# A two-block model layer: eight of twelve w_mod column blocks pre-summed on GpSimd, then summed over rows by TensorE

## The reference, cut to what matters

```
mod_x = jnp.split((jax.nn.silu(c) @ w_mod + b_mod)[:, None, :], 6, axis=-1)
mod_c = jnp.split((jax.nn.silu(c_ctx) @ w_mod + b_mod)[None, None, :], 6, axis=-1)
hc = modulate(rmsnorm(ctx, norm1_g), mod_c[0], mod_c[1])
hx = modulate(rmsnorm(x, norm1_g), mod_x[0], mod_x[1])
```

## Time and profile before

| | |
|---|---|
| median of 3 runs | 1835.47 us (1831.92 to 1836.16) |
| span of the profiled execution | 1824.3 us; no time of its own is recorded beside it |
| TensorE matmul / VectorE / ScalarE / GpSimd busy | 93% / 35% / 24% / 9% |
| mean granted TensorE clock | 0.969 |
| w_mod stage (first w_mod product to start of attention) | 105.75 to 202.04 us |

### The profile page before, as it was taken

One profiled execution on the slowest core, in us unless ns is written; L12 is line 12 of the kernel. 1 busy time (PEld: TensorE's weight loads), 2 busy tenths in 40 slices (PEclk: granted clock), 3 DMA queues, 4 the chain that ended last, 5 costly groups with the idle time before them and its releaser, 6 DMA issues.

```text
span 1824.3 us, 21872 instructions
## 1 busy us (share of the span) xinstructions
PE 1705.0 (93%) x8774; PEld 885.3 (49%) x8774; DVE 647.0 (35%) x1210; ACT 443.7 (24%) x775; POOL 170.2 (9%) x172
## 2 busy tenths in 40 slices
PE   7999999889999999999699998999799999999983
PEld 3455564545445555455355548975433333333331
DVE  3379111242223122221269947542522221222213
ACT  2233552214312122111258512331100000000001
POOL 0000000011111111110000023100111111111110
PEclk9999999989999999999899999999799999999997
DMA  9274611389999999999480091044799999999994
GB/s 367 93 257 160 213 70 47 133 321 407 392 401 411 407 400 406 407 411 413 174 322 1 5 143 47 1 162 194 277 392 403 406 409 407 406 421 408 417 414 175
DMA packets 94220, 515.26 MB, mean 282 GB/s; under 512 B 22429, under 2 KB 28157, under 8 KB 69544
## 3 DMA queue, kind: packets, MB, share of 16 engines
q1 hardware_dynamic: 82920, 496.46, 70.0%
q0 software_dynamic: 11200, 17.39, 2.9%
HBM read 506.09 MB, written 27.05 MB: 292 GB/s over the span
## 4 chain that ended last, share of the span: by engine, by line
PE 70%; DMA 15%; issue 7%; DVE 5%; SPq 2%; ACT 1%; DVEq 0%; POOLq 0%
PE bank L852 22%; PE bank L868 10%; PE bank L454 8%; PE bank L462 8%; DMA ring<-in_w_up 7%; DMA ring<-in_w_down 4%; PE bank L809 3%; PE bank L839 3%; PE bank L730 2%; PE bank L879 2%; PE bank L520 2%; PE bank L685 2%; PE bank L447 1%; DVE arena L2549 1%; DMA ring<-diag 1%
## 5 line engine op out<-in xcount | busy, mean ns | idle before, releaser
L854 PE MATMUL bank<-ring,arena 128*64 128x512 f32 x928 | 418.7, 605 | 0.0
L852 PE MATMUL bank<-ring,arena 128*64 128x512 f32 x752 | 339.1, 604 | 9.4 <-DMA ring<-in_w_up 6.8
L868 PE MATMUL bank<-ring,arena 128*64 128x512 f32 x544 | 247.9, 598 | 2.6 <-DMA ring<-in_w_down 2.6
L870 PE MATMUL bank<-ring,arena 128*64 128x512 f32 x544 | 247.9, 598 | 0.0
L2448 DVE TENSOR_TENSOR arena<-arena,bank 64x512 f32<-64x512 f32 x70 | 48.3, 690 | 560.5 <-ACT arena L1763 560.5
L454 PE MATMUL bank<-arena,ring 128*128 128x512 f32 x560 | 244.6, 593 | 0.0
L852 PEld LDWEIGHTS bank<-ring,arena 128*64 128x64 f32 x752 | 100.7, 139 | 208.5 <-issue 202.4
L852 PE MATMUL bank<-arena 128*64 128x512 f32 x368 | 166.1, 605 | 9.3 <-DMA ring<-in_w_up 5.0
L1429 POOL DMA_INDIRECT arena<-xnd,smalli x70 | 67.6, 966 | 1074.4 <-PE bank L839 536.0
L454 PEld LDWEIGHTS bank<-arena,ring 128*128 128x128 f32 x560 | 105.2, 190 | 127.2 <-issue 127.2
L1763 ACT ACTIVATE arena<-bank 64x512 f32<-64x512 f32 x70 | 41.2, 588 | 512.1 <-PE bank L854 512.1
(11 more groups left out here) (439 smaller groups left out, 1999.2 us busy)
## 6 DMA issues: line engine op xcount, KB each, us to landing
ring<-in_w_down SPq DMA_DIRECT2D x62, 2048.0 KB, 33.2
ring<-in_w_up SPq DMA_DIRECT2D x54, 2048.0 KB, 16.9
ring<-in_w_gate SPq DMA_DIRECT2D x45, 2048.0 KB, 17.4
arena<-in_w_gate SPq DMA_DIRECT2D x19, 2048.0 KB, 25.2
ring<-in_w_mod SPq DMA_DIRECT2D x12, 2048.0 KB, 8.0
ring<-in_w_in SPq DMA_DIRECT2D x10, 2048.0 KB, 15.7
arena<-in_w_up SPq DMA_DIRECT2D x10, 2048.0 KB, 29.8
ring<-in_w_out SPq DMA_DIRECT2D x4, 2048.0 KB
```

Source lines behind the costliest of these rows:

```text
L852: pe.matmul(GU[0:CAP, :], x, wg_[:, c, :], start=(c == 0), stop=(c == KD - 1), skip_group_check=True)
L854: mm = pe.matmul(GU[CAP:2 * CAP, :], x, wu_[:, c, :], start=(c == 0), stop=(c == KD - 1), skip_group_check=True)
L868: pe.matmul(Y[0:CAP, :], x, wd_[:, c, 0:512], start=(c == 0), stop=(c == 3), skip_group_check=True)
L870: mm = pe.matmul(Y[CAP:2 * CAP, :], x, wd_[:, c, 512:1024], start=(c == 0), stop=(c == 3), skip_group_check=True)
```

## The change

Of the twelve w_mod blocks, the eight whose columns only mod_x needs (2048 to 6143) are now taken first, and the four that both vectors need come last (`MOD`). For the first eight (`SUMMED`), GpSimd multiplies each of the 8 chunks of a landed block by that chunk's column of silu(c), in place, then adds chunks 4 to 7 onto 0 to 3, 2 to 3 onto 0 to 1, and 1 onto 0. TensorE then needs 4 products for the block instead of 32: the 128 partitions of chunk 0 against a stationary pair of columns, ones and zeros. It waits for GpSimd's sum first. The other four blocks go as before. The places move: blocks 6 and 7 (counted from 1) stand after the last q/k feature, blocks 8 to 10 behind the first value tile; 11 and 12 stay.

```diff
+        only_first = small(2)
-        for n, u in enumerate(U_MOD):
-            plain[u] = cols(a["w_mod"], n)
+        MOD = [4, 5, 6, 7, 8, 9, 10, 11, 0, 1, 2, 3]
+        SUMMED = 8
+        for i, u in enumerate(U_MOD):
+            plain[u] = cols(a["w_mod"], MOD[i])
...
-            def modulation(n0, n1):
+            def modulation(i0, i1):
-                for n in range(n0, n1):
-                    w = use(U_MOD[n])
+                for i in range(i0, i1):
+                    n = MOD[i]
+                    w = use(U_MOD[i])
                     b = V.deal(pe, f"mod{n}")
-                    for k in range(KD):
+                    if i < SUMMED:
+                        pe.wait_ge(S("mod_summed"), i + 1)
                         for g in range(4):
-                            mm = pe.matmul(b[32 * g:32 * g + 2, 0:P], chunks(cs, 2)[:, k, :], w[:, k, P * g:P * g + P],
-                                           start=(k == 0), stop=(k == KD - 1), skip_group_check=True)
+                            mm = pe.matmul(b[32 * g:32 * g + 2, 0:P], only_first, w[:, 0, P * g:P * g + P],
+                                           start=True, stop=True, skip_group_check=True)
+                    else:
+                        ...
-            pe.wait_ge(S("consts"), 3)
+            pe.wait_ge(S("consts"), 4)
...
-            modulation(5, 9)
+            modulation(5, 7)
...
-                    modulation(9, 10)
+                    modulation(7, 10)
...
-            sp.wait_ge(V.free, V.at("mod11"))
+            sp.wait_ge(V.free, V.at(f"mod{MOD[-1]}"))
...
+            pool.wait_ge(S("silu_c"), 1)
+            for i in range(SUMMED):
+                pool.wait_ge(*landed(U_MOD[i]))
+                w = unit(U_MOD[i])
+                for k in range(KD):
+                    pool.tensor_scalar(w[:, k, :], w[:, k, :], cs[:, 2 * k:2 * k + 1], None, ALU.mult)\
+                        .then_inc(S("mod_scaled"), 1)
+                pool.wait_ge(S("mod_scaled"), KD * (i + 1))
+                pool.tensor_tensor(w[:, 0:4, :], w[:, 0:4, :], w[:, 4:8, :], ALU.add).then_inc(S("mod_added"), 1)
+                pool.wait_ge(S("mod_added"), 2 * i + 1)
+                pool.tensor_tensor(w[:, 0:2, :], w[:, 0:2, :], w[:, 2:4, :], ALU.add).then_inc(S("mod_added"), 1)
+                pool.wait_ge(S("mod_added"), 2 * i + 2)
+                pool.tensor_tensor(w[:, 0, :], w[:, 0, :], w[:, 1, :], ALU.add).then_inc(S("mod_summed"), 1)
...
+            dve.memset(only_first[:, 0:1], 1.0)
+            dve.memset(only_first[:, 1:2], 0.0).then_inc(S("consts"), 1)
...
```

More of the change, by code:

```diff
@@ L623, in context @@
                         four(CV, "SU", si, z[ZC[10]], z[ZC[6]])
-            def modulation(n0, n1):
-                for n in range(n0, n1):
-                    w = use(U_MOD[n])
+            def modulation(i0, i1):
+                for i in range(i0, i1):
+                    n = MOD[i]
+                    w = use(U_MOD[i])
                     b = V.deal(pe, f"mod{n}")
-                    for k in range(KD):
+                    if i < SUMMED:
+                        pe.wait_ge(S("mod_summed"), i + 1)
                         for g in range(4):
-                            mm = pe.matmul(b[32 * g:32 * g + 2, 0:P], chunks(cs, 2)[:, k, :], w[:, k, P * g:P * g + P],
-                                           start=(k == 0), stop=(k == KD - 1), skip_group_check=True)
+                            mm = pe.matmul(b[32 * g:32 * g + 2, 0:P], only_first, w[:, 0, P * g:P * g + P],
+                                           start=True, stop=True, skip_group_check=True)
+                    else:
+                        for k in range(KD):
+                            for g in range(4):
+                                mm = pe.matmul(b[32 * g:32 * g + 2, 0:P], chunks(cs, 2)[:, k, :],
+                                               w[:, k, P * g:P * g + P],
+                                               start=(k == 0), stop=(k == KD - 1), skip_group_check=True)
                     mm.then_inc(V.full, 1)
-                    used(U_MOD[n], V, f"mod{n}")
+                    used(U_MOD[i], V, f"mod{n}")
             b = C.deal(pe, "ss_x")
-            pe.wait_ge(S("consts"), 3)
+            pe.wait_ge(S("consts"), 4)
             for k in range(0, KD, 2):
@@ L2117, in _, with modulation @@
             chain(TS(gq8, pcol("gq"), HD ** -0.5, None, ALU.mult))
-            def modulation(n0, n1):
-                for n in range(n0, n1):
+            def modulation(i0, i1):
+                for n in MOD[i0:i1]:
                     b = take(f"mod{n}")
```

## The result

The changed kernel takes 1884.36 us (median of 4 runs, 1883.16 to 1888.81) against 1835.37: ratio 1.0274, 95% interval 1.0258 to 1.0290, 49 us slower. 1861.5 had been forecast, with 1844 to 1883 as the range. The direction is right, the size is almost double, and the time lies outside the range. The loss also came by another path than the one forecast.

What follows compares the result with a forecast made beforehand. TensorE was taken as the bound, with VectorE 0.8 us behind in the w_mod stage. VectorE's hold by GpSimd gave +24.8, low clock and unit 11's wait +1.5: +26 on 1835.5, 1861.5 us, range 1844 to 1883.

Steps and rivals of the forecast that it cites:

- the multiply lies between 0.54 and 1.22; I take 0.65: GpSimd's 128x512 multiply by a column, eight per w_mod unit: 0.65 us each, giving 13.2 us a unit with the adds.
- GpSimd by itself is just quick enough: GpSimd's sums of w_mod units: 1 to 5 end by 101 us, 6 to 8 by 158, in time for TensorE.
- the point of change itself: If taps are not held, the result stays near 1834 as long as GpSimd's unit is under 14.4 us.
- the rival in which GpSimd becomes the bound: Multiply takes 1.00 us, a unit 16 us bare and 21 beside VectorE; q/k features wait: +42, 1877 us; chance 0.2.
- The forecast's own upper end: With a multiply of 1.22 and adds of 8.5 us, a unit costs VectorE 14.6 us: +46.
- 36 us of hold: VectorE between 77.9 and 176 us: five units at 9.6 us, 48 us, times a share of 0.75.
- VectorE loses T - 0.33 for each GpSimd instruction it meets: Taps and norms wait for a whole GpSimd instruction of length T; a unit costs VectorE 9.6 us.
- The forecast's 0.32: VectorE's taps and norms: loss of 0.32 us for each GpSimd multiply met, eight per unit.
- What TensorE is spared: Eight w_mod units with 4 products instead of 32: 12.9 us less work, of which 1.5 us was taken to stay.
- The low clock behind a long wait: TensorE after a long wait: 1.9 us on a q/k feature, 1.8 us on the column sum behind the taps.
- the marks named: Signs of being right: slow taps, 320 w_mod records, column sum waiting near 200, multiply 0.5 to 0.8, q/k sum late.
- the sign of being wrong: Taps at 0.75 us beside GpSimd, or TensorE waiting for GpSimd rather than VectorE.

Runs made afterwards that it cites:

- Run 3: Changed kernel with GpSimd's multiply by a column operand replaced by one of two tensors, the second being that column repeated 512 times: 1870.71 us, ratio 1.0215.
- run 6: Changed kernel with 58 of the convolution's 62 taps left out on VectorE: 1876.97 us, ratio 1.0240.
- run 2: Changed kernel with GpSimd's multiplies taken out, so it only adds the unscaled chunks of the eight blocks: 1845.52 us, ratio 1.0070.
- run 1: Changed kernel with GpSimd's adds taken out, so it only multiplies and TensorE sums 8 chunks with 32 products again: 1830.11 us, ratio 0.9990.
- run 7: Changed kernel with only the first three w_mod blocks summed by GpSimd, using the two-tensor multiply: 1832.95 us, ratio 1.0004.

## Why the prediction was wrong

- **The term that failed is "the multiply lies between 0.54 and 1.22; I take 0.65".** It took 1.54 from start to start alone, and 1.70 on average in the whole run: above the upper bound. The bounds came from another engine and from two-input products, with the thought that one input costs less. Run 3 shows the contrary in this very place: two tensors 1.00 us, one tensor and a column 1.54. What the GPSIMD Engine Reference of the Trainium skill ("Engine selection") says, roughly line-rate for one input (0.43 us as an estimate), does not hold here: 3.6 times as long was measured, and the measurement decides.
- **With it fell "GpSimd by itself is just quick enough".** The step's arithmetic was right: 36.9 + 8 x 20.65 gives 202 us for the eighth sum if GpSimd never rests; it came at 207 in run 6 and at 216 in the changed kernel. The prediction had the point of change itself (14.4 us a block), but gave the rival in which GpSimd becomes the bound 0.2. That rival's condition is what happened. Its sum is not: it has 46.5 us of hold on VectorE and 4 of waits for sums, where the trace has 60.7 us of such waits. That its 1877 lies near 1884 is in part luck. The forecast's own upper end (+46, at 18.3 us a block) counted no wait for a sum either, though 18.3 lies above its own 14.4.
- **The path was another one.** The prediction let VectorE be late and TensorE behind it. In the changed kernel GpSimd is on the path, and it is held too: 64 multiplies cost 9.2 us more than 64 x 1.54, the adds 4.6 more than bare. That is the 13.8 us from 202.1 to 216. VectorE's lateness is real (its 60 taps took 83.4 us instead of 45.1) and of about the size forecast (36 us of hold), but it ends 1.6 us ahead of its use.
- **"VectorE loses T - 0.33 for each GpSimd instruction it meets"** was right for the adds (run 2: 7.0 us for each of two blocks, forecast 7.1) and agrees with run 3 (+38, expected 33 to 43), and was wrong for the multiplies of this kernel. With their true 1.54 it would give 1.21 us for each; in run 1 all 60 taps together lost 5.9 us beside some 40 multiplies, 0.15 for each. The forecast's 0.32 was nearer to this than its rule deserved: the multiply too short and its hold too strong cancelled in that term, by luck.
- **What TensorE is spared**: 12.9 us of work gone is right, and nothing of it arrives. In run 7 (4.8 gone, 0 won) VectorE's copies cover it, as the prediction said; in the changed kernel TensorE only waits for GpSimd that much longer.
- **The low clock behind a long wait**: it came behind the second, third and fourth wait, and only the last is on the path: 1.9 us (5.64 for two blocks of 1.86 from 216.52), which is about what the prediction put down once.
- Of the marks named, the taps "with one of over 4 us" came, and w_mod's 320 records (24 + 5 x 8 and 128 + 2 x 64). The first column sum of q/k was not late: it starts at 89.84, 0.5 us after the 89.35 of before, as the whole timeline is by then. The column sum over the taps did not wait for VectorE. The multiply was not at 0.5 to 0.8. That TensorE waited for GpSimd rather than VectorE was named as the sign of being wrong, and it is the one that counts.

What stays open: why GpSimd's one-input multiply is slower than the two-tensor one and yet hardly holds VectorE. It may be the column operand; no run here separates that. What the changed kernel would lose if only its sums came in time is not shown either: VectorE would bound it next, and run 3, with the shorter chain and the stronger hold, still lost 38 us.

## What to carry to other kernels

An engine that gets its first work of a kind needs that kind's duration from a row of the same operation and operands; a row of another form is no bound, on either side. Work moved to an idle engine makes a chain of its own: multiply its length per item by the items and set the end against the moment of use before pricing anything else. And GpSimd's two-tensor instructions held VectorE's instructions with two SBUF inputs, and some with one, until they were done (not the reciprocal and not the copies out of PSUM), so in this kernel they belong where VectorE reads PSUM or rests.

## What was not expected of the hardware

- On GpSimd, 128x512 float32: multiply by a column operand 1.54 us, multiply by that column repeated as a tensor 1.00 (both from start to start); durations of the add of two tensors 1.26 us, of the adds of 1024 and 2048 columns 2.34 and 4.51.
- Beside a two-tensor instruction of GpSimd a tap of VectorE took up to 4.97 us; beside a 1.54 us multiply with a column operand it took 0.90 instead of 0.75 on average.
- A VectorE tensor-scalar instruction of 128x1024 SBUF to SBUF took 5.00 us instead of 0.69 beside a GpSimd add of 2048 columns; a reciprocal of the same size was untouched.
- After the same wait of 2.14 us TensorE's next block took 3.71 us in one execution and 2.23 in another (granted clock 0.57 and 1.00 in the two microseconds from 115): differences of 1.5 us between two kernels need not come from their edits.
